# The gated delta layer's q and k norms, moved into and ahead of the memory attention

## The reference, cut to what matters

```python
q, k, v = jnp.split(jax.nn.silu(qkv).astype(jnp.float32), 3, axis=-1)
q = _l2norm(q.reshape(b, s, DN_HEADS, DN_HEAD_DIM)) * (DN_HEAD_DIM ** -0.5)
k = _l2norm(k.reshape(b, s, DN_HEADS, DN_HEAD_DIM))      # t * rsqrt(sum(t*t) + EPS)
...
o_fwd = _gated_delta_chunked(q, k, v, g[:, :, 0], beta[:, :, 0])
o_bwd = rev(_gated_delta_chunked(rev(q), rev(k), rev(v), rev(g[:, :, 1]), rev(beta[:, :, 1])))
...
mem_out = _memory_attention(q_mem, mem_n, w_mem_kv)      # k, v = split(mem_n @ w_kv); softmax over 256 memory tokens
return jnp.concatenate([o, mem_out], axis=-1) @ w_out
```

## Time and profile before

| | |
|---|---|
| median of 3 runs | 2932.04 us (2931.57 to 2935.28) |
| the profiled execution's own time | 2930.64 us |
| its span, first to last instruction | 2928.5 us |
| mean granted TensorE clock | 0.935 of 2.4 GHz |
| PE busy | 2623.7 us, 90% of the span |
| PEld, DVE, ACT, POOL busy | 73%, 49%, 36%, 9% |
| the stretch at issue | 2106 us (end of the memory's projection) to 2166 us (first head) |

### The profile page before, as it was taken

The page is one execution under the profiler, slowest core; times in us unless marked ns, Lnnn a source line. Parts: engine busy times, 40 slices in busy tenths (PEclk is TensorE's granted clock), DMA queues, the critical chain, the costliest instruction groups (busy, mean ns, idle before and its releaser), DMA issues.

```text
span 2928.5 us, 33226 instructions
## 1 busy us (share of the span) xinstructions
PE 2623.7 (90%) x13178; PEld 2125.6 (73%) x13178; DVE 1449.2 (49%) x2374; ACT 1068.6 (36%) x1873; POOL 268.6 (9%) x420
## 2 busy tenths in 40 slices
PE   6898999999789989999789999999778687899998
PEld 4677777788357777877468888888547676688887
DVE  5667565653484556532335333257445555443422
ACT  3445432422463455444424222242433333332221
POOL 5233021020000132000000000010000100000000
PEclk7999999999799999999789999999779788999999
DMA  5522273364012311330103333232200000233332
GB/s 207 180 71 88 80 253 128 102 218 141 30 37 73 130 37 58 107 91 30 44 29 108 101 94 95 87 116 83 68 1 1 1 1 1 65 94 101 94 94 79
DMA packets 146227, 250.16 MB, mean 85 GB/s; under 512 B 15455, under 2 KB 65914, under 8 KB 145049
## 3 DMA queue, kind: packets, MB, share of 16 engines
q1 hardware_dynamic: 129008, 198.08, 21.8%
q0 software_dynamic: 14816, 48.31, 5.0%
q10 hardware_dynamic: 2249, 1.65, 0.2%
HBM read 245.84 MB, written 5.30 MB: 86 GB/s over the span
## 4 chain that ended last, share of the span: by engine, by line
PE 75%; DVE 10%; ACT 8%; DMA 4%; issue 2%; POOL 0%; SPq 0%; DVEq 0%; ACTq 0%
PE PS L218 19%; PE PS L220 18%; PE PS L219 18%; PE PS L985 2%; ACT tmp L752 1%; PE PS L2314 1%; PE PS L2317 1%; DMA hT_b<-in_w_mod 1%; PE PS L2327 1%; PE PS L2324 1%; PE PS L1760 1%; ACT w_hi L203 1%; PE PS L1445 1%; DVE x L808 1%; PE PS L1744 1%
## 5 line engine op out<-in xcount | busy, mean ns | idle before, releaser
L210 DVE TENSOR_TENSOR w_lo<-w_raw,w_hi 128x1024 fp32r<-128x1024 f32 (+1 forms) x344 | 412.5, 1206 | 779.1 <-ACT w_hi L203 777.9
L203 ACT ACTIVATE w_hi<-w_raw 128x1024 fp32r<-128x1024 f32 (+1 forms) x344 | 356.6, 1045 | 1039.3 <-DMA w_raw<-in_ffn_w_gate_up 308.0
L218 PE MATMUL PS<-hT_hi,w_hi 128*128 128x512 f32 (+1 forms) x1728 | 661.0, 383 | 21.5 <-DVE hT_lo L820 13.7
L220 PE MATMUL PS<-hT_hi,w_lo 128*128 128x512 f32 (+1 forms) x1728 | 652.7, 378 | 0.0
L219 PE MATMUL PS<-hT_lo,w_hi 128*128 128x512 f32 (+1 forms) x1728 | 652.3, 378 | 0.0
L218 PEld LDWEIGHTS PS<-hT_hi,w_hi 128*128 128x128 f32 x1728 | 331.0, 192 | 85.1 <-issue 19.3
L220 PEld LDWEIGHTS PS<-hT_hi,w_lo 128*128 128x128 f32 x1728 | 330.4, 191 | 59.4
L219 PEld LDWEIGHTS PS<-hT_lo,w_hi 128*128 128x128 f32 x1728 | 331.0, 192 | 56.8 <-issue 0.2
L218 PE MATMUL PS<-w_hi,hT_hi 128*128 128x512 f32 (+1 forms) x704 | 289.9, 412 | 35.3 <-DVE hT_lo L2722 9.1
L219 PE MATMUL PS<-w_lo,hT_hi 128*128 128x512 f32 (+1 forms) x704 | 278.4, 395 | 0.0
L220 PE MATMUL PS<-w_hi,hT_lo 128*128 128x512 f32 (+1 forms) x704 | 278.0, 395 | 0.0
(11 more groups left out here) (546 smaller groups left out, 3546.9 us busy)
## 6 DMA issues: line engine op xcount, KB each, us to landing
w_raw<-in_ffn_w_gate_up SPq DMA_DIRECT2D x176, 256.0 KB, 3.1
mraw<-in_w_mod POOLq DMA_DIRECT2D x160, 256.0 KB, 4.0
w_raw<-in_gla_w_in SPq DMA_DIRECT2D x48, 512.0 KB, 4.7
w_raw<-in_ffn_w_down SPq DMA_DIRECT2D x44, 512.0 KB, 3.8
w_raw<-in_fox_w_in SPq DMA_DIRECT2D x32, 512.0 KB, 4.3
w_raw<-in_sgu_w_in SPq DMA_DIRECT2D x24, 512.0 KB, 4.7
w_raw<-in_dn_w_in SPq DMA_DIRECT2D x24, 512.0 KB, 3.6
w_raw<-in_gla_w_out SPq DMA_DIRECT2D x16, 512.0 KB, 4.5
```

What stands on the lines that cost most here:

```text
L203: nc.scalar.activation(w_hi[:, n % NS, :, 0:m], w_raw[:, n % NS, :, 0:m], ACT.Copy).then_inc(w_hidone, 1)
L210: nc.vector.tensor_tensor(w_lo[:, n % NS, :, 0:m], w_raw[:, n % NS, :, 0:m], w_hi[:, n % NS, :, 0:m].bitcast(F32), ALU.subtract).then_inc( ...
L218: nc.tensor.matmul(o, l_hi, r_hi, start=start, stop=False)
L220: return nc.tensor.matmul(o, l_lo, r_hi, start=False, stop=stop)
```

## The change

`norm_heads` is no longer called in this layer; its work is written out in small functions and put elsewhere (fox_layer still calls it).

- Squares: all twelve go on ACT right behind `act_feed(ahead(kv))` and ahead of the copies of the keys and values, into twelve tiles of their own (hT_a and hT_b), so that no square waits for a sum.
- Sums: on PE right behind the memory's projection, in bank 2, ahead of the gate sums; then the square root on ACT ahead of the three exponentials, and reciprocal and split on DVE behind L2642 and ahead of the first unit's maximum. The scores of the first unit also wait for the square root, which frees bank 2.
- Spreads 0 to 6: one at every second unit (u = 2, 4, ..., 14), on PE in the hook between the values and the turns, on DVE in the hook behind the scale of u-1. They use bank 7.
- Spreads 7 to 11: behind the memory units as before, in banks 0 and 1.

```diff
-            nh = norm_heads(Group(sq=L0, sum=2 * L0, root=1, rows=1, nrm=L0), 2 * NH, 1, 2, (0, 1), r.sums,
-                            lambda n: d_.AT[:, 0, n % 2, :], tile, lambda n: 1.0 if n % 2 else float(P) ** -0.5,
-                            (d_.TT[:, 0, 0, :], hT_hi[:, 5, :], hT_lo[:, 5, :]),
-                            lambda n: identr[0:2 * NH, n:n + 1].to_broadcast([2 * NH, P]))
+            square = lambda n: (hT_a, hT_b)[n // KT][:, n % KT, :]
+            rr, rhi, rlo = hT_b[0:2 * NH, 6, :], hT_hi[0:2 * NH, 5, :], hT_lo[0:2 * NH, 5, :]
+            NM = 7
+            spread_bank = lambda n: 7 if n < NM else (n - NM) % 2
+
+            def lengths_pe():
+                t_ = nc.tensor
+                for n in range(2 * NH):
+                    t_.wait_ge(lens.sq, L0 + n + 1)
+                    t_.matmul(PS[0:2 * NH, 2, :], r.sums[:, 2 * NH - n:4 * NH - n], square(n), start=n == 0,
+                              stop=n == 2 * NH - 1).then_inc(lens.sum, 1)
+
+            def normed_pe(n):
+                t_ = nc.tensor
+                t_.wait_ge(lens.rows, 2)
+                if 0 < n < NM or n >= NM + 2:
+                    t_.wait_ge(lens.nrm, L0 + (n if n < NM else n - 1))
+                for m, z in enumerate((rhi, rlo)):
+                    mm = t_.matmul(PS[:, spread_bank(n), :], identr[0:2 * NH, n:n + 1].to_broadcast([2 * NH, P]), z,
+                                   start=m == 0, stop=m == 1)
+                mm.then_inc(lens.sum, 1)
+
+            def squares_act():
+                for n in range(2 * NH):
+                    nc.scalar.activation(square(n), tile(n), ACT.Square).then_inc(lens.sq, 1)
+
+            def lengths_act():
+                nc.scalar.wait_ge(lens.sum, 2 * L0 + 2 * NH)
+                nc.scalar.activation(rr, PS[0:2 * NH, 2, :], ACT.Sqrt, bias=eps[0:2 * NH]).then_inc(lens.root, 1)
+
+            def lengths_dve():
+                v = nc.vector
+                v.wait_ge(lens.root, 2)
+                then_dve(v.reciprocal(rr, rr))
+                then_dve(v.tensor_copy(rhi, rr))
+                v.tensor_tensor(rlo, rr, rhi.bitcast(F32), ALU.subtract).then_inc(lens.rows, 1)
+
+            def normed_dve(n):
+                nc.vector.wait_ge(lens.sum, 2 * L0 + 2 * NH + n + 1)
+                nc.vector.scalar_tensor_tensor(out=tile(n), in0=tile(n), scalar=1.0 if n % 2 else float(P) ** -0.5,
+                                               in1=PS[:, spread_bank(n), :], op0=ALU.mult, op1=ALU.mult).then_inc(lens.nrm, 1)
+
+            def between_units(step):
+                def at(u):
+                    if u % 2 == 0 and 2 <= u < 2 * NM + 2:
+                        step(u // 2 - 1)
+                return at
...
+                t_.wait_ge(q.gdve, 3)
+                lengths_pe()
                 t_.wait_ge(ps_evac, kv.ev)
-                t_.wait_ge(q.gdve, 3)
...
-                mem.pe([(q.mask, 4)])
+                mem.pe([(q.mask, 4), (lens.root, 2)], between=between_units(normed_pe))
                 t_.wait_ge(su.po, 10)
-                nh.pe()
+                for n in range(NM, 2 * NH):
+                    normed_pe(n)
...
                 act_feed(ahead(kv))
+                squares_act()
...
+                lengths_act()
...
-                nh.act(tile)
...
-                mem.dve()
-                nh.dve()
+                lengths_dve()
+                mem.dve(between_units(normed_dve))
+                for n in range(NM, 2 * NH):
+                    normed_dve(n)
```

## The result

| | before | after |
|---|---|---|
| median of 4 runs each | 2932.12 us (2931.57 to 2935.28) | 2953.47 us (2951.95 to 2956.78) |
| ratio after / before, 95% interval | | 1.0072 (1.0055 to 1.009) |
| the profiled execution's own time | 2930.64 us | 2956.78 us |
| its span, mean granted clock | 2928.5 us, 0.935 | 2954.7 us, 0.924 |

The change makes the kernel 21 us slower. The forecast was 2941, with a range of 2934 to 2948 of its own and of 2931 to 2952 for 8 in 10: right in sign, too small in size, and 1.5 us outside the wider range.

A forecast was written before the change was run, and what follows sets the result against it. PE stands for 75% of the chain; the norms alone take 30.6 us before the first head. -26.2 behind the units + 16.7 ahead + 21.9 between - 1.3 - 0.9 = +10.2 us, so 2941 us, range 2934 to 2948.

The forecast's parts named there:

- Squares not under the projection: Ahead of the units: ACT's squares wait behind the last weight chunk, starting 2.6 us after PE finishes the memory's projection.
- Sums 12.2 us (10.5 to 13.8): Ahead of the units: PE's twelve sums take 12.2 us, 10.5 at full clock, 13.8 with four at twice the time.
- From the sums to the first maximum 7.2 us: Ahead of the units: square root, table load, exponentials with negation, reciprocal and split run one behind the other, 7.2 us.
- The closed loop: Between units: DVE's multiplication waits for PE's spread, making each pair a round trip of 4.74 us full clock, 6.6 half.
- rival 4: Between units: PE's spread is done before DVE's multiplication, so the maximum isn't late; faster, about 2920 or 2925 us; chance 0.12.
- The clock, 0.71: In the units: PE's mean clock 0.71, from the attention layer's units, giving 5.7 us a pair and 21.9 us lost.
- rival 3: In the units: half clock throughout, pairs losing 28.2 us, net +19.6, so about 2951 us; chance 0.14.
- Five spreads 4.4 us: Behind the units: the five remaining spreads take 4.4 us, between 3.7 at full clock and 5.0 at half.
- Small terms: Behind the units and in the first head: one table load off the path wins 1.3 us, faster gate matmuls 0.9.

The follow-up runs named there:

- e5: Changed kernel with ACT's twelve squares ahead of the rounding of the output projection's weight chunks; 2944.86 us, ratio 1.0052 to the kernel before.
- e1: Changed kernel with no spread between the memory units, all twelve behind them; 2929.39 us, ratio 0.9996 to the kernel before.
- e3: Changed kernel with seven unread matmuls filling PE's wait for the reciprocal, ahead of the first scores; 2947.34 us, ratio 1.0052 to the kernel before.
- e4: Changed kernel with seven unread matmuls in PE's wait for the reciprocal and one behind each of the seven spreads; 2935.12 us, ratio 1.0016 to before.
- e11: Changed kernel again, unaltered, on another chip job; 2951.09 us, ratio 1.0056 to the kernel before.
- e10: Changed kernel with one unread matmul behind each spread between the units, none during the reciprocal; 2942.24 us, ratio 1.0037 to the kernel before.
- e2: Changed kernel with DVE's multiplication by a spread two units later in its queue, PE's order unchanged; 2934.42 us, ratio 1.0011 to the kernel before.
- e9: Kernel before, with only the memory's row norms moved ahead of the gates' activations; 2923.99 us, ratio 0.9974 to the kernel before.

## Why the prediction was right in sign and short in size

The first sentence of each point is the step as it was predicted, the second what was found.

- **Squares not under the projection.** Predicted at 1.1 us behind the start of the last weight chunk, 2.6 behind the projection. They came 1.0 behind the one and 2.0 behind the other; e5, which moves them, brings the first maximum 2.8 to 4.1 us nearer (predicted 3).
- **Sums 12.2 us (10.5 to 13.8).** 10.5 here (2118.63 to 2129.09), at clock 1.00, after 2.79 us of idle PE; in e1, after 3.13 us, 12.2. In e3, with more of them at the half clock, it is 13.4. Nearly the whole of the bound occurred, and the value that I chose was another run's.
- **From the sums to the first maximum 7.2 us.** 7.1: root 0.68, load 1.28, exponentials and negation 0.66, reciprocal and split 4.4, one behind the other. With the earlier squares and the shorter sums the first maximum comes 14.5 later, where 16.7 was predicted.
- **The closed loop.** Predicted 4.74 us a pair at full clock and 6.6 at half. Measured 4.71 (e4) and 6.44 (after); the wait view names the spread seven times, as it should. At the half clock it is 0.61 from the multiplication to the maximum, 0.94 to the turns, 2.58 to the values, 1.06 to the spread and 1.25 to the next multiplication, where 0.69, 0.95, 2.58, 1.13 and 1.25 were predicted. The chain was right term by term, and rival 4 (no late hook) fell.
- **The clock, 0.71.** This is the step that failed. The clock was 0.50 for all of the units. From the first turns to the last it is 44.5 us (2137.87 to 2182.33: six pairs of 6.44 and a last one of 5.82), for 18.0 before. So the seven pairs cost 26.5 us where 21.9 were predicted, and the units as a whole 27.4. That is near the 28.2 of rival 3, to which I gave 0.14. I took the 0.71 from the attention layer's units because PE was busy for 33.3 of 48 us there. Here it was busy for 35.5 of 48.1 and got 0.50: a like share of busy time did not bring a like clock.
- **Five spreads 4.4 us.** 5.3, the bound at the half clock (5.0) and the handover.
- **Small terms.** The table load in front of the first head's exponentials is gone, as predicted; from the first head to the second it is 44.9 us for 45.5 (44.2 in e11), so 0.7 to 1.3 were won. The gate matmuls' 0.9 weren't: they still take 3.78, at the half clock.

Why this stretch held 0.50 and the attention layer's did not is open. It is not that PE has no gaps there. That stretch, in the kernel before, keeps PE waiting for DVE's scale once a pair too, and for longer:

```profile
1469.21 0.44 PE L1751 MATMUL PS<-ident,att_P 128*128 128x128 f32 x2 [2.17 <-DVE att_P L1819]
...
1476.65 0.44 PE L1751 MATMUL PS<-ident,att_P 128*128 128x128 f32 x2 [2.41 <-DVE att_P L1819]
```

Six such gaps, of 2.07 to 2.41 us, lie between 1451 and 1491, and the clock went up and down around them, between 0.64 and 0.76 over parts of the stretch of 7 us and more. So a gap in every pair does not by itself give 0.50. What the experiments show is this loop's case: with a gap of 1.59 us in every pair of 6.44 the clock stayed down or fell (the changed kernel, e3, e5, e11), and with the gaps filled (e4, e10) or gone (e2) it stayed up or came back.

From the measured terms, 14.5 and 27.4 more and 25.3 less are +16.7 before rounding, with the 0.7 of the first head +16.0, so 2948 from the median of before. The medians say +21.3 and, in e11's company, +18.4 (2951.09 less 2932.66). The 2 to 5 us above lie outside the stretch. Upstream the profiles move by as much (e11), but that it was so in these runs is not shown. With the measured sizes in the forecast's own sum it is 10.2 - 2.2 (first maximum) + 5.5 (units) + 0.9 (five spreads) + 0.6 (table load) + 0.9 (gate matmuls) = 15.9. So of the 11.1 us between the forecast's +10.2 and the +21.3, the units are the largest part that has a name, with 5.5 (4.6 of them the pairs' clock), and 5.4 are not located. That the first maximum was put 2.2 us too late hid some of it, which was luck.

The Trainium skill (TensorE: Matmul & The Clock Gate, "Why this matters for your kernels") names PE-idle gaps over about 3 us as what brings the half clock. I leaned on it. The changed kernel's wait of 5.65 us for the reciprocal agrees with it, since the half clock follows. It is not enough here: in e3 the clock fell in a gap of 1.59 us with none longer in the 26 us ahead, and in the changed kernel gaps of that length went with 0.50 for 48 us. Its section "A second HAM failure mode: psum-queue depth-cycling" comes nearer, with frequent short idles between groups of matmuls under which the clock goes up and down. The attention layer's 0.71 agrees with that; in the changed kernel's pairs the profile shows it staying down. By measurement, e4 and e10 settle that filling the gaps keeps it up or brings it back.

## What to carry to other kernels

When an instruction is put between two stages of a software pipeline, walk its operand back through the engines: if it needs something that an engine issues only behind the work that the next stage is to release, two half loops become one, and the cost per turn is a whole round trip, not the instruction. Moving it later by one turn (a pair of units here) on the waiting engine alone opens the loop again (e2). Price such a loop at both clocks, and if PE has a gap in every turn, give the slow one a large chance: here it held throughout. The mean clock of another stretch, which had gaps too, misled. Then test by filling the gaps with matmuls that nothing reads, which tells the clock's part from the loop's. And compare two profiles from a point ahead of the edit, not by their spans: e9's gain of 8.8 us looked like 4.3 until the shift upstream was taken out.

## What the runs showed of the hardware that I had not expected

- Added work can save time: seven matmuls of 128x512 ahead of the units and one in each pair brought the changed kernel from 1.0072 (1.0056 in e11) to 1.0016 (e4) of before.
- The same seven pairs hold either clock. With their gaps of 1.59 us they stayed at 0.50 for 48 us, though PE was at work for most of the time, and in e3 they lost a full clock that they began with; with a fill in each (e4) they stayed at 1.00 for 35 us.
- A reciprocal of 12x512 takes DVE 3.33 us, while a multiplication of 128x512 takes 0.69. Few partitions save nothing: the heads' reciprocals of 128x512 (DVE, six of them in the kernel before) take 3.35 us each. This one instruction is over half of PE's wait of 5.65 us ahead of the units.
